# DeltaNet's chunk front in a hybrid decoder layer: decay sums and key scales brought over the partitions by DMA instead of by TensorE

## What is computed

```python
gc = cumsum(g within a chunk)                       # decay sums, per head
kb, vb = kc * beta, vc * beta
decay = exp(where(incl, gc[..., :, None] - gc[..., None, :], -inf))
M = where(strict, (kb @ kc^T) * decay, 0)           # A = I + M, solved against [vb, kb*exp(gc)]
qk = (qc @ kc^T) * decay
k_dec = kc * exp(gc[..., -1:] - gc)
# then, chunk after chunk, with the state S of each head:
v_new = u - w @ S;  o = (qc*exp(gc)) @ S + qk @ v_new;  S = S*exp(gc_last) + k_dec^T @ v_new
```

## Time and profile before

| | |
|---|---|
| median of 3 runs | 1625.77 us (1624.47 to 1627.68) |
| the profiled execution | 1627.18 us, its span 1625.4 us |
| TensorE busy | 1592.6 us, 98% of the span |
| VectorE, ScalarE, GpSimd busy | 883.1, 578.5, 648.7 us |
| granted TensorE clock, mean | 0.997 of full speed |

### The profile page before, as it was taken

The page is one execution under the profiler, slowest core; times in us unless marked ns, Lnnn a source line. Parts: engine busy times, 40 slices in busy tenths (PEclk is TensorE's granted clock), DMA queues, the critical chain, the costliest instruction groups (busy, mean ns, idle before and its releaser), DMA issues.

```text
span 1625.4 us, 20530 instructions
## 1 busy us (share of the span) xinstructions
PE 1592.6 (98%) x7955; PEld 1327.0 (82%) x7955; DVE 883.1 (54%) x1326; ACT 578.5 (36%) x838; POOL 648.7 (40%) x477
## 2 busy tenths in 40 slices
PE   7999999999999999999999999999999999999998
PEld 4888888888888888888788887788888888878886
DVE  5322222454536353566554148756666565878886
ACT  4422221123222243333222134444444444444445
POOL 3334322312131223224324347987788888000111
PEclk9999999999999999999999999999999999999999
DMA  5232332121213042335367031422234433686575
GB/s 171 66 94 88 115 97 61 43 69 39 69 38 81 27 125 71 99 113 154 122 209 269 14 110 35 135 91 91 91 98 122 124 108 94 232 306 218 195 263 183
DMA packets 204172, 192.24 MB, mean 118 GB/s; under 512 B 23364, under 2 KB 156972, under 8 KB 204076
## 3 DMA queue, kind: packets, MB, share of 16 engines
q1 hardware_dynamic: 203856, 190.85, 37.8%
q10 hardware_dynamic: 220, 0.09, 0.0%
HBM read 142.57 MB, written 48.33 MB: 117 GB/s over the span
## 4 chain that ended last, share of the span: by engine, by line
PE 91%; DVE 4%; DMA 2%; issue 1%; POOL 1%; SPq 1%; ACT 0%; DVEq 0%; ACTq 0%
PE acc L562 37%; PE acc L2469 12%; PE bank_ab L1408 7%; PE bank_ab L2469 6%; PE acc L2479 6%; PE att_ps L2469 5%; PE att_ps L2479 3%; PE bank_ab L2479 3%; PE acc L1843 3%; PE att_ps L1483 2%; PE bank_ab L1843 1%; PE att_ps L1843 1%; PE att_ps L1465 1%; DVE u_t_full L1799 1%; PE att_ps L1476 1%
## 5 line engine op out<-in xcount | busy, mean ns | idle before, releaser
L562 PE MATMUL acc<-xh,w_high 128*128 128x512 f32 x832 | 276.9, 409 | 0.6 <-POOL xl L1732 0.6
L562 PE MATMUL acc<-xl,w_high 128*128 128x512 f32 x832 | 262.1, 392 | 0.0
L562 PE MATMUL acc<-xh,w_low 128*128 128x512 f32 x832 | 261.1, 390 | 0.0
L973 POOL TENSOR_TENSOR w_low<-w_raw,w_high 128x1024 fp32r<-128x1024 f32 x49 | 117.4, 2395 | 346.8 <-ACT w_high L1055 346.8
L562 PEld LDWEIGHTS acc<-xh,w_low 128*128 128x128 f32 x832 | 156.5, 188 | 34.2
L562 PEld LDWEIGHTS acc<-xl,w_high 128*128 128x128 f32 x832 | 156.6, 188 | 33.9
L562 PEld LDWEIGHTS acc<-xh,w_high 128*128 128x128 f32 x832 | 147.2, 189 | 27.0 <-issue 3.8
L1146 ACT ACTIVATE sc<-sc,mx 128x128 f32<-128x128 f32 (+1 forms) x96 | 35.5, 441 | 173.4 <-DVE mx L1352 173.4
L1246 DVE SCALAR_TENSOR_TENSOR cs<-acc,prm,cs 128x1023 f32<-128x1023 f32 (+2 forms) x36 | 46.1, 1281 | 77.0 <-ACT cs L1073 76.2
L2245 POOL TENSOR_TENSOR f_h<-f_h,f_fw 128x512 f32<-128x512 f32 x8 | 10.9, 1368 | 175.1 <-ACT f_junk L2168 175.1
L2479 PE MATMUL acc<-f_w_high,f_gh 128*128 128x512 f32 x176 | 69.6, 395 | 3.5 <-DVE f_gl L2333 3.5
(11 more groups left out here) (386 smaller groups left out, 3828.1 us busy)
## 6 DMA issues: line engine op xcount, KB each, us to landing
w_raw<-in_w_in_dram SPq DMA_DIRECT2D x51, 512.0 KB, 4.6
f_raw<-glu_d SPq DMA_DIRECT2D x66, 256.0 KB, 3.1
f_raw<-in_w_down_dram SPq DMA_DIRECT2D x55, 256.0 KB, 4.0
w_raw<-in_w_up_dram SPq DMA_DIRECT2D x24, 512.0 KB, 5.2
glu_d<-u_free_high SPq DMA_DIRECT2D x22, 512.0 KB, 4.6
u_raw_even<-in_w_up_dram SPq DMA_DIRECT2D x20, 512.0 KB, 4.7
f_raw<-gsum_d SPq DMA_DIRECT2D x33, 256.0 KB, 3.5
conv_d<-so SPq DMA_DIRECT2D x16, 512.0 KB, 3.0
```

What stands on the lines that cost most here:

```text
L562: mm = nc.tensor.matmul(out[:, lo:hi], w, xx[:, lo:hi], start=first and j == 0, stop=last and j == 2)
L973: g.tensor_tensor(wl[:, n % 2], raw[:, n % 2], wh[:, n % 2].bitcast(F32), ALU.subtract).then_inc(s_wlo, 1)
```

## The change

Three things are changed together.

- Once, early: `gatesum` makes two more products, with a new matrix Um (U less one in its upper 64 rows), the decay sums counted from the chunk's middle, once as columns (kept in `g_all`, sign changed) and once as rows of 32 partitions. A new item `rowsT` in job 12 transposes `nbr` to rows by one more product. ScalarE copies both out, SyncE stores them to DRAM (`rows_d`).
- Each chunk: one DMA (`load_spread`) brings the chunk's rows of sums and of scales, 2x4x128 numbers, to all 128 partitions (`spread`, 512 KB written, in the room of `o_stage`). It is issued behind the 8 stores of the chunk before.
- The stage kT is gone. VectorE makes XB from the untransposed keys in SBUF and `spread`. GpSimd subtracts the sums from a mask, ScalarE takes exp with the column's sum as bias, one instruction for each head, GpSimd multiplies by rk. The product with `Ls` and the multiplication by U are gone. kkD moves from behind T4 to before it, and the loop of a chunk is one slot shorter; the slots before the first chunk keep their number (kt one slot later).

```diff
     def front(c):
-        return [[(name, c)] for name in ("kt", "kT", "kkD")]
+        return [[(name, c)] for name in ("kt", "kkD")]
...
-        out += [("vq", c)] + kt + [("P4", c)] + kT + [("T4", c)] + kkD + rest + [("P5", c)] + ml + [("T5", c)] + ob + sv0
+        out += [("vq", c)] + kt + [("P4", c)] + kkD + [("T4", c)] + rest + [("P5", c)] + ml + [("T5", c)] + ob + sv0
...
+            if kind == "conv" and t == 3 * NH - 1 and k == 4:
+                items.append(("rowsT",))
...
+        Um = nc.alloc_sbuf_tensor_at("Um", [P, P], F32, offset=rows_at[-1])
+        spread = stage_o[:].rearrange("p a h c -> p (a h c)").rearrange("p (a h c) -> p a h c", a=2, h=NH)
...
+            def load_spread(c):
+                if c:
+                    sp.wait_ge(s_gu, 2 * c - 1)
+                    sp.wait_ge(s_a, a_taken[("kt", c - 1)])
+                sp.dma_start(spread, rows_d[:, c, :].rearrange("j (h t) -> j h t", h=NH).unsqueeze(0)
+                             .to_broadcast([P, 2, NH, P])).then_inc(s_rl, 16)
...
+                if kind == "rowsT":
+                    sp.wait_ge(s_attk, att_no[("gatesum",)])
+                    sp.wait_ge(s_attk, att_no[it])
+                    for j in range(2):
+                        sp.dma_start(rows_d[j].rearrange("c (h t) -> (c h) t", t=P), rows_t[j][0:NT * NH, :]
+                                     ).then_inc(s_rst, 16)
...
                     if name == "load":
+                        sp.wait_ge(s_rst, 48)
+                        load_spread(0)
...
                             sp.dma_start(m_d[c, b].rearrange("h j i -> j h i"), WT[c % 2][own, :, own]).then_inc(s_md, 16)
+                        if c + 1 < NT:
+                            load_spread(c + 1)
...
+            step(g.tensor_copy(Um[:], U[:]))
+            step(g.tensor_scalar(Um[0:P // 2, :], U[0:P // 2, :], -1.0, None, ALU.add))
             g.memset(tiny[:], 0.0).then_inc(s_tri, 1)
...
-                        if c == 0:
-                            pool.wait_ge(s_gready, 1)
-                        else:
+                        pool.wait_ge(s_rl, 16 * (c + 2))
+                        if c:
                             pool.wait_ge(s_a, a_taken[("vq", c - 1)])
-                            pool.wait_ge(s_dtm, 2 * c)
-                        g.tensor_tensor(DTr[:], bh(U[:]), bc(g_all[:, c, :]), ALU.mult).then_inc(s_gu, 1)
+                        g.tensor_tensor(DTr[:], bh(amask[:, 0:P]), spread[:, 0], ALU.subtract).then_inc(s_gu, 1)
                     if name == "kkD":
-                        pool.wait_ge(s_b, b_taken[(name, c)])
-                        g.tensor_tensor(DTr[:], DTr[:], bh(U[:]), ALU.mult).then_inc(s_dtm, 1)
-                        pool.wait_ge(s_dtm, 2 * c + 1)
+                        pool.wait_ge(s_gu, 2 * c + 2)
                         g.tensor_tensor(DTr[:], DTr[:], bc(rr[:, 1, :, c]), ALU.mult).then_inc(s_dtm, 1)
...
-                    if name == "kT":
-                        act.wait_ge(s_dn, dn_done[(name, c)])
-                        g.activation(XB[:], A4, ACT.Copy).then_inc(s_a, 1)
                     if name == "kkD":
-                        act.wait_ge(s_dn, dn_done[(name, c)])
-                        g.activation(DTr[:], B4, ACT.Exp).then_inc(s_b, 1)
+                        act.wait_ge(s_gu, 2 * c + 1)
+                        for h in range(NH):
+                            ins = g.activation(DTr[:, h, :], DTr[:, h, :], ACT.Exp, bias=g_all[:, c, h:h + 1])
+                        ins.then_inc(s_gu, 1)
...
-                        g.tensor_tensor(XB[:], A4, bc(nbr[:, c, :]), ALU.mult)
+                        dve.wait_ge(s_rl, 16 * (c + 2))
+                        g.tensor_tensor(XB[:], ckqk[c % 2][:, NH:2 * NH, :], spread[:, 1], ALU.mult)
...
-                    if name == "kT":
+                    if name == "kkD":
                         pe.wait_ge(s_a, a_taken[("kt", c)])
-                        last = each_head(A4, XB, None, True)
-                    if name == "kkD":
-                        pe.wait_ge(s_a, a_taken[("kT", c)])
-                        pe.wait_ge(s_gu, c + 1)
-                        each_head(A4, kc, XB)
-                        last = t_.matmul(bank_b[:, :], Ls[:], DTr[:].rearrange("p h c -> p (h c)"), start=True,
-                                         stop=True)
+                        last = each_head(A4, kc, XB)
```

More of the change, by code:

```diff
@@ L89, in dn_stages @@
     ml, sv0, sv1, sv2, ts, tl, ex = solving(0)
-    out = [("load", 0)] + rest * 3 + sum(front(0), []) + rest * 2 + ml + rest + sv0 + rest * 3 + sv1 + sv2 + rest
+    out = [("load", 0)] + rest * 4 + sum(front(0), []) + rest * 2 + ml + rest + sv0 + rest * 3 + sv1 + sv2 + rest
     out += ts + rest + tl + rest * 2 + ex + rest
     for c in range(NT):
-        kt, kT, kkD = front(c + 1) if c + 1 < NT else (rest, rest, rest)
+        kt, kkD = front(c + 1) if c + 1 < NT else (rest, rest)
         ml, sv0, sv1, sv2, ts, tl, ex = solving(c + 1) if c + 1 < NT else [[]] * 7
         ob = [("ob", c - 1)] if c else []
-        out += [("vq", c)] + kt + [("P4", c)] + kT + [("T4", c)] + kkD + rest + [("P5", c)] + ml + [("T5", c)] + ob + sv0
+        out += [("vq", c)] + kt + [("P4", c)] + kkD + [("T4", c)] + rest + [("P5", c)] + ml + [("T5", c)] + ob + sv0
         out += [("P6", c)] + sv1 + [("kS", c)] + sv2 + ts + [("T6", c), ("vn", c)] + tl + [("so", c)] + ex
@@ L201, in build @@
     gsum_d = nc.dram_tensor("gsum_d", [FT, P, HALF], F32, kind="Internal").ap()
+    rows_d = nc.dram_tensor("rows_d", [2, NT, NH * P], F32, kind="Internal").ap()
     m_d = nc.dram_tensor("m_d", [NT, NBLK, NH, BASE, BASE], F32, kind="Internal").ap()
@@ L244, in build @@
         mixed, places, ready = mixer(nc, sem, sb, acc, bank_ab, att_ps, ident, ones, prm, small, xh, xl, xd,
-              norm1_w, norm2_w, dn_conv_w, ffn_conv_w, ffn_conv_b, w_in2, dn_a_log, dn_dt_bias, dn_onorm_w, conv_d, og_d, ob_d, gate_d, m_d, t_d,
+              norm1_w, norm2_w, dn_conv_w, ffn_conv_w, ffn_conv_b, w_in2, dn_a_log, dn_dt_bias, dn_onorm_w, conv_d, og_d, ob_d, gate_d, rows_d, m_d, t_d,
               w_pa2, w_pb2, ring, m_ring, g_ring, s_rows)
@@ L586, in mixer @@
     job_no = {(kind, t): n for n, (kind, t, _) in enumerate(jobs)}
-    use_a = {"kt", "kT", "kkD", "vq", "P4", "T4", "P5", "T5", "P6", "kS", "vn", "so", "ob"}
-    use_b = {"kkD", "vq", "T4", "T5", "T6", "kS", "so"}
+    use_a = {"kt", "kkD", "vq", "P4", "T4", "P5", "T5", "P6", "kS", "vn", "so", "ob"}
+    use_b = {"vq", "T4", "T5", "T6", "kS", "so"}
     dn = [it[1:] for it in items if it[0] == "dn" and it[1] not in OFF_PE]
@@ L594, in mixer @@
     b_taken = count([d for d in dn if d[0] in use_b])
-    att_no = count([it for it in items if it[0] in ("gates", "gatesum", "vT", "a_qk", "a_pT", "a_pv", "cmbT")])
+    att_no = count([it for it in items if it[0] in ("gates", "gatesum", "rowsT", "vT", "a_qk", "a_pT", "a_pv", "cmbT")])
     order = {it: n for n, it in enumerate(items)}
@@ L623, in mixer @@
     s_ckqk, s_ckv, s_ckz = [sem("m_chunk_qk0"), sem("m_chunk_qk1")], sem("m_chunk_v"), sem("m_chunk_z")
+    s_rst, s_rl = s_rows[4], s_rows[5]
     s_gu, s_dtm, s_scale = sem("m_gu"), sem("m_decay_masked"), sem("m_row_scales")
@@ L701, in mixer @@
             fold = sb(early, "fold", [P, 2 * NH])
+            rows_t = [sb(early, f"rows_t{j}", [P, P]) for j in range(2)]
         oh_at = ol_at + NBR * S * 4
@@ L883, in x_sync @@
                     c = it[1]
+                    if c == 0:
+                        sp.wait_ge(s_gu, 2 * NT - 1)
+                        sp.wait_ge(s_a, a_taken[("kt", NT - 1)])
                     sp.wait_ge(s_obst, 16 * (c + 1))
@@ L1301, in x_vector @@
                     if name == "kkD":
-                        dve.wait_ge(s_dtm, 2 * c + 2)
+                        dve.wait_ge(s_dtm, c + 1)
                         if c >= 2:
@@ L1448, in x_tensor @@
                     pe.wait_ge(s_tri, 1)
-                    for j, m in enumerate((U, Ls, ones)):
+                    for j, m in enumerate((U, Ls, ones, Um)):
                         last = t_.matmul(att0[:, j * NT * NH:(j + 1) * NT * NH], m[:],
                                          g_all[:].rearrange("p c h -> p (c h)"), start=True, stop=True)
+                    last = t_.matmul(att0[0:NT * NH, P:2 * P], g_all[:].rearrange("p c h -> p (c h)"), Um[:],
+                                     start=True, stop=True)
                     last.then_inc(s_atpe, 1)
+                if kind == "rowsT":
+                    pe.wait_ge(s_scale, 1)
+                    t_.matmul(att0[0:NT * NH, 0:P], nbr[:].rearrange("p c h -> p (c h)"), ident[:], start=True,
+                              stop=True).then_inc(s_atpe, 1)
                 if kind == "vT":
```

5 lines of the change are left out of this document (added).

## The result

| | before | after |
|---|---|---|
| median, the two run in turns on one chip | 1626.83 us (1624.47 to 1630.0) | 1630.55 us (1627.82 to 1634.84) |
| ratio | | 1.0026 (95% interval 1.0018 to 1.0034) |
| the profiled execution, its span | 1627.18, 1625.4 us | 1627.82, 1626.1 us |
| TensorE busy | 1592.6 us | 1583.0 us |

The account below looks back on a forecast made before the run. TensorE's own work was taken to set the time; -9.9 us of work, +5.0 of new waits and -2.0 of old ones gave -6.9, a span of 1618.5 and a median of 1618.9 us; range 1612 to 1626.5.

Parts of the forecast that it names:

- the bound: Whole kernel: TensorE's own work sets the time; a stage costs how far it pushes the next job matmul.
- what is removed and added: On TensorE: kT's transposes 3.6 us and the product with Ls 7.0 removed, three small products 0.7 added; net -9.9.
- the three new waits: TensorE at T4 behind kkD(5), T4 behind kkD(6) and P4 behind kt(7): 1.7, 1.2 and 1.6 us.
- What moves, and which waits it makes: Mixer's stage order: 14-slot chunks drift over attention's items; new waits +5.0 us, old waits -2.0.
- the gap at 707.44 goes: Combination: kkD(7)'s gap, 1.5 us of idle, goes because kkD(7) now lies before attention's end.
- The gap at 777.15 stays: Combination: gap of 2.3 us with a slower clock behind it stays, since ob, combination and w_low meet again at ob(6).
- small ones: Stages with a_pv followed one step later, as so(3) and T5: new waits of together 0.5 us.
- B: Rival: XB meets GpSimd's subtraction or w_low in most chunks, waits eat nearly all; 1622.5 to 1626 us; chance 0.21.
- C: Rival: the mask is ready no sooner than before, waits at T4 together 14.4 us; +4.1, 1629.9 us; chance 0.08.
- D: Rival: spread load or what it delays holds an engine 1 us in seven chunks; 1625 us or little less; chance 0.03.
- The skill's rule: At XB: a VectorE instruction with two SBUF inputs contends with a GpSimd instruction reading SBUF, one waiting out the other.

Follow-up runs that it names:

- 15-slot kernel: The kernel after with 15 slots for each chunk, an empty slot where kT stood and kkD behind T4 again: 1617.05 us, ratio 0.9937.
- run with one row: Against the 15-slot order of 1617.05 us: spread loads of chunks 1 to 7 cut to one partition, chunk 0's sums used throughout; ratio 0.9937.
- e0_after: The kernel after, unedited, run again as anchor of the slot experiments: 1630.02 us, 1.0022 of the kernel before.

## Why the prediction was wrong, by its steps

**Right: the bound, and what is removed and added.** TensorE sets the time; 10.6 us less and 0.7 more were forecast, -9.9. The 15-slot kernel, which has all of it in the old places, measures this without the breaks. Between the same two job matmuls, those at 186.94 and 729.23 us of before, it takes 10.97 us less, and 0.5 of that is a shorter break (1.24 at 567.75 where before had 1.71 at 707.44): 10.5 us removed. `rowsT` adds the 0.56 us by which every kernel with the new front takes longer between the job matmuls at 154 and 187 us; what `gatesum` adds does not stand out from the scatter of the first 90 us. The whole span of that kernel is 10.1 us shorter.

**Right: the three new waits.** Forecast 1.7, 1.2 and 1.6; measured 1.79, 1.43 and 1.12. The row of T4 behind kkD(6) in after, released by WT:

```profile
609.92 0.69 DVE L1339 TENSOR_TENSOR d_WT<-bank_ab,d_DTr 128x512 f32<-128x512 f32 x1 [1.32 <-issue]
610.66 0.60 PE L1441 MATMUL bank_ab<-d_P,d_U 128*128 128x128 f32 x3 [1.36 <-DVE d_WT L1339]
```

At kt(7) XB started when w_low ended (665.02) and took 0.68, kd 0.68, and GpSimd's subtraction beside them took 1.79. It was not XB itself that waited out w_low, as the prediction has it, but the small copy ahead of it (L1394), which lasted 1.91 us there in place of 0.16.

**Wrong: "What moves, and which waits it makes".** The step saw that 14 is no multiple of three and that "its stages drift over a_qk, a_pT and a_pv". It then followed only the stages that the change edits, kkD and kt, and asked only who holds DeltaNet's own banks. The other stages drift as well, and they hold something else: VectorE's time, between attention's scores and their exponentials. That is 4.15 us of a_pT, of which the run without the inverse gives 3.7 back.

**Wrong: "the gap at 707.44 goes".** kkD(7) did leave it, but so(6) came in: in after its state update (L1361, 713.74) and output addition stand ahead of the same combination, and the small steps L1410, L1411 and L1413 last 1.01, 0.98 and 0.78 us in place of 0.17 beside GpSimd's steps, and the scaling of the groups then meets w_low (against the earlier trace rows for the break):

```profile
718.58 2.39 POOL L1006 TENSOR_TENSOR w_low<-w_raw,w_high 128x1024 fp32r<-128x1024 f32 x1
718.68 3.24 DVE L1416 TENSOR_TENSOR qk<-qk,cbs 128x256 f32<-128x256 f32 x3
...
722.98 0.41 PE L1529 MATMUL att_ps<-ident,PT 128*128 128x128 f32 x2 [1.08 <-DVE PT L1424]
```

1.27 us by starts in place of 1.71. I removed one cause of the break and did not ask what takes its slot. That so(6) is the new cause is read from the timeline; the run with chunks 6 and 7 on the old places, which moves it away, has this break no more.

**Missed: the break at 786.69.** With the last chunk's stages ending earlier, ob(7) falls beside a later combination; the scaling of the groups (L1416) lasts 3.04 us and the next addition (L1423) 2.50, beside GpSimd's steps of ob and osplit and then w_low. 2.56 us, and 1.5 more of half clock behind it. "The gap at 777.15 stays" held: 3.24 at 752.27, where before had 2.63.

**The miss in numbers.** Forecast span 1618.5, measured 1626.1: 7.6 us. Not forecast: 4.15 at a_pT, 1.27 at 722.98, 4.1 at 786.69 with its half clock, together 9.5. Against it stand 0.2 of the three waits, 0.3 of small ones, 0.3 more of work and 0.5 regained behind 811 us; 0.6 stays unassigned. In medians the miss is 11.7 us (1630.55 for 1618.9). The other 4 are the step from the span to the runs' median, put at 0.4 and measured at 4.4: the profiled execution is the lowest of 20. What makes the other runs longer no profile shows.

**The rivals.** B (XB meets GpSimd in most chunks) is out: XB took 0.68 to 0.69 us in six chunks, 1.82 in one (302.5) and 1.52 in one (519.0), and TensorE waited for neither. C (T4 waits in every chunk) is out: two waits for WT, not seven; that its 1629.9 us lies beside the measured 1630.55 is luck. D is out: the run with one row is no faster, and between 200 and 811 us after's TensorE waits for neither a load nor `w_high`. A rival for a cost outside the edited stages was missing, and the case for "slower" had only C's chance.

**The skill's rule.** The Trainium skill, SBUF — State Buffer, "Who interferes with whom", was weighed for XB. It holds on this trace (XB at 302.5 lasts 1.82 us beside GpSimd), but the price was elsewhere. The same section of the Trainium skill says that a `copy` whose operands meet certain conditions can enter a mode that takes the ports shared with GpSimd. The trace agrees: the copy of four numbers a row (L1394) lasts 0.16 us alone and 2.37 beside w_low, just ahead of an a_qk.

## What to carry to other kernels

In a list that every engine walks in order, the number of slots of a loop is a parameter of its own: where two loops interleave, a whole ratio keeps every stage in the same slot of the other loop, but it must be the right slot (the same 15 slots moved by one lost 8.5 of 10.2 us). Keep number and phase, or go through all stages of both loops that share an engine, not only the edited ones. Whether another order of 14 slots would keep the gain was not run. When work is taken out, put a rest in its slot first (here: 1617.05 us instead of 1630.02), and shorten the loop as a separate step with its own measurement. An engine that is busy half of the time still decides when it stands between two steps of the one that is full.

## What the runs showed of the hardware

The clock behind a break is not a function of the break. Two executions of the same kernel, the kernel after and its repeat `e0_after`, have the same wait of 2.3 us for ckz near 752 us; windows of 752 to 757 us, of the first and of the second:

```profile
752.00:757.00 5.00, 4.73 (x19) 3.96 (x20) 0.91 (x2) 0.35 (x2) 0.00 (x0) 0.66 0.73 218
```

```profile
752.00:757.00 5.00, 3.93 (x22) 3.41 (x23) 2.13 (x4) 0.90 (x2) 0.15 (x1) 1.00 0.58 161
```

A granted clock of 0.66 over these five us is a stretch at 1.2 GHz within 2.4 GHz; in the second it never fell. A wait of 1.08 us (the kernel with one slot more ahead of P6(7)) was followed by such a stretch too, and in its sister not. The kernel with one row loaded has the same two waits, and there the clock fell behind the one of 1.1 us and stayed up behind the one of 2.3. Each stretch costs 1.5 to 2 us by starts. The kernel after, with more breaks, spreads over 7.0 us of run times where before spreads over 5.5; that the clock makes this difference is not shown. A single profile of a kernel with breaks of one to three us is therefore uncertain by a few us, more than many changes are worth.
